# Down-weight loads split over two queues, and an earlier evacuation between retention heads

## The chip, the cores and the metric

The kernel runs on one core of a Trainium2 chip. The metric is the device time of one launch in microseconds. The three runs of the kernel before took 4532.19, 4537.35 and 4538.72 us, median 4537.35.

## The reference, cut to what matters

One inference step of a decoder layer over 576 tokens (512 prompt tokens and 8 sequences of 8 new tokens), width 2048, everything in float32. In order: a mixer (pooling groups beside four retention heads), attention over 256 memory tokens, and a channel mixer with 16384 one-neuron experts, of which every token uses 8 x 16.

```python
def retention_mixer(q, k, v, gate, pos, s0, ret_norm_g):
    ...
    qh = rotary(heads(q), pos)
    kh = rotary(heads(k), pos) * (RET_HEAD_DIM ** -0.5)
    o, s_new = retention_seq(qh, kh, vh, s0.astype(F32))
    ...
    return jax.nn.silu(gate.astype(F32)) * o, s_new

def peer(h, peer_wq, peer_subkeys, peer_u, peer_v):
    ...
        u = jnp.take(peer_u, expert, axis=0).astype(F32)
        act = jax.nn.gelu(jnp.einsum('thkd,td->thk', u, xb.astype(F32)), approximate=False)
        vv = jnp.take(peer_v, expert, axis=0).astype(F32)
        return jnp.einsum('thk,thkd->td', g * act, vv).astype(h.dtype)
```

## The kernel before, in words

**Split products.** TensorE multiplies in float32r. Each operand is split into a high part (the value rounded to float32r) and a low part (the rest), and a product is three matmuls: high by high, high by low, low by high. Weights arrive in chunks of 512 KB (128 partitions x 1024 floats). A chunk k goes through slot k % 4: a DMA fills the raw slot, ScalarE writes the high part to WS (helper `high`, L1086, the copy is recorded at L1080), and POOL subtracts to make the low part (`low_part`, L482, L484). When the low part is done, the raw slot is free for chunk k + 4. In the expert quads DVE makes the low parts of every fourth chunk, slot 3 (`low_last`, L2162, L2165).

**Retention.** Four heads, in a loop of three and a last one. TensorE projects eight blocks per head (`head_block`, L720, 96 matmuls each at L598): two of queries, two of keys, two of gates and two of values for the next head; between them stand the transposes and products of the head. ScalarE's `retention` (L1313) issues the load of the decay tables and eight loads of states, and calls `evac_head(h, 0)` (L1279), which waits for the block, evacuates it and makes the high parts of the weights two blocks on. Then it copies the transposed values, evacuates the other blocks, stores the new states, takes a square root, stores the mixer's output (L1353) and waits for its stores to land before the next head.

**Expert quads.** For most tokens (320 of 576) all experts are computed densely, four blocks of 128 experts at a time: a quad. The up weights of the first ten blocks of map rows were done earlier, so 27 quads (i = 0 to 26, QT = 27) hold 16 chunks each: 0 to 7 are up weights (uT), 8 to 15 down weights (vE), two chunks for each of four quarters q of the output. TensorE (`up`, L1016; `down`, L1033) runs four up projections, each of 48 matmuls at L598 and ended by a gelu on ScalarE, and then the down product, 16 output blocks d of 12 matmuls each at L1045. Quarter q of it waits for the low parts of chunks 8 + 2q and 9 + 2q. DVE adds each output block to X (`sums`, L2143, L2150) and, after block d = 1 and d = 9, makes the low part of chunks 11 and 15. Five more quads (27 to 31) have down weights alone.

The other 256 tokens use gathered rows: POOL issues ten gathers of 1 MB per quad (L517) in quads 0 to 25 between its low parts, and DVE multiplies and adds them (L2135).

**Queues.** SP issues every weight load, in the order of the chunks, each behind a wait for its slot (`slot_free`, L426: POOL's semaphore for slots 0 to 2, DVE's for slot 3). ScalarE's queue takes the stores of gelu values (L1551, 160 KB each, four per quad) and, in `load_next` (L1620), the two 640 KB loads for the next quad: the map of gates (PP from pmap, L1611) and the gelu values (GI, L1613). In quad 0 it takes the last stores of the map as well (L1574). POOL's queue has the gathers.

**ScalarE's order in a quad** is `ups` (L1624): for each of the four up blocks (a, e) the evacuation `gelu_out` (L1542), which also makes the high parts of the two chunks four places on (blocks (0,0), (0,1), (1,0), (1,1): chunks 4 and 5, 6 and 7, 8 and 9, 10 and 11), then the gelu store; load_next follows block (1, 0). Behind `ups` come four steps `next_highs` (L1652) with the high parts of 12 and 13, 14 and 15, and of the next quad's 0 to 3.

Of the kernel before, what the change touches and what calls it, by code (L numbers as in the profile page):

```python
# [97 lines left out]
def used(n):  # L98


    return n + 4
# [12 lines left out]
def split_uv(i12, k):  # L114

    assert k % 4 < 3
    return i12 + (H_UV + 5 + k // 4 * 3 + k % 4)


def low_uv(i4, k):  # L120

    return i4 + (k // 4 + 2)
# [37 lines left out]
def build(nc, xT, memT, w_lin, gains, consts, spoolT, sret, kcT, vc, pool_w, rot, tabs, subk, uT, vE,  # L160
          yT, npoolT_p, nret_p, mkT, mv, npoolT_s, nret_s):
    with ExitStack() as ctx:
# [3 lines left out]
        def sem(name):  # L166
            return ctx.enter_context(nc.semaphore(name))
# [50 lines left out]
        def raw(k, many, late=False):  # L218

            if late and k >= 2:  # L220
                return CS.rearrange("p a t -> p (a t)")[:, 0:HW] if k == 2 else RAW3
            return RAW[:, k, :] if k < 2 else RAWX[:, k - 2, :] if many else RAW[:, k - 2, :]
# [96 lines left out]
        S = {n: sem(n) for n in names}  # L319
# [19 lines left out]
        def _(sp):  # L339
# [98 lines left out]
                                 uT.rearrange("(b x) p w -> x b p w", x=2)[k // 4, bass.ds(4 * quad, 4), :, 256 * (k % 4):256 * (k % 4 + 1)]  # L438
                                 .rearrange("b p w -> p b w")).then_inc(S[f"raw{k % 4}"], 16)

            def load_v(i, i12, i4, first):

                for q in range(4):
                    for b in range(2):
                        k = first + 2 * q + b
                        slot_free(i12, i4, k)
                        sp.dma_start(raw(k % 4, True, True).rearrange("p (e d) -> p e d", e=2),
                                     vE[bass.ds(i * 4 + 2 * b, 2), :, 512 * q:512 * (q + 1)].rearrange("e p d -> p e d"))\
                            .then_inc(S[f"raw{k % 4}"], 16)
# [12 lines left out]
            with sp.Fori(0, QT) as i:  # L462
                for k in range(8):
                    slot_free(i * 12, i * 4, k)
                    sp.dma_start(raw(k % 4, True, True), uT[bass.ds(i * 8 + (4 * LAG + k), 1)].rearrange("a p n -> p (a n)"))\
                        .then_inc(S[f"raw{k % 4}"], 16)
                load_v(i, i * 12, i * 4, 8)
            with sp.Fori(0, NQ - QT) as i:
                load_v(i + QT, i * 6 + 12 * QT, i * 2 + 4 * QT, 0)
            for s in range(2):  # L470
# [608 lines left out]
        def _(act):  # L1079
# [163 lines left out]
            for b in range(SB):  # L1243
                r, q = b // 4, b % 4
# [34 lines left out]
            def evac_head(h, m):  # L1279
                act.wait_ge(S["used"], h * 16 + used(H_HEAD + 2 * m + 2))  # L1280
                if HEAD[m] in (4, 5):
                    pad_values(HEAD[m] - 4, m % 2)
                kw = {"scale": RD ** -0.5} if m in (2, 3) else {}
                act.activation(halves(RAWQ[:, HEAD[m], :]), pair(m % 2), ACT.Silu if m in (4, 5) else ACT.Identity, **kw)\
                    .then_inc(S["lin_evac"], 1)
                high2(h * 16 + (H_HEAD + 2 * m + 4), 2 * (m % 2))
# [26 lines left out]
            def retention(h, more):  # L1313
                act.dma_start(TAB, tabs[bass.ds(h, 1)].rearrange("a p n -> p (a n)")).then_inc(S["in_tab"], 16)
                for b in range(SB):
                    act.dma_start(SST[:, b], sret[b, bass.ds(h, 1)].rearrange("a (c p) v -> p (a c) v", p=P))\
                        .then_inc(S["in_st"], 16)
                evac_head(h, 0)
                act.wait_ge(S["vt_done"], h + 1)
                copy(VTOK[:, 0:4, :], PS[:, 2048:3072].rearrange("p (t n) -> p t n", t=4))  # L1320
                copy(VTOK[:, 4, :], bank(6, RD)).then_inc(S["v_evac"], 1)
                for m in range(1, 5):
                    if m == 4:
                        act.wait_ge(S["b_done"], h + 1)
                    evac_head(h, m)
                act.wait_ge(S["kt_done"], h + 1)
                act.wait_ge(S["in_tab"], h * 16 + 16)
                for t in range(4):
                    copy(KTOK[:, t, :], PS[:, 2048 + RD * t:2048 + RD * (t + 1)], scale=TAB[:, T_ZETA + t:T_ZETA + t + 1])
                copy(KTOK[:, 4, :], bank(6, RD)).then_inc(S["k_evac"], 1)  # L1330
                evac_head(h, 5)
                if more:
                    evac_head(h, 6)
                else:
                    act.wait_ge(S["rot_done"], RH)
                    act.wait_ge(S["used"], used(H_OUT))
                    split_early(mixT, Z_OUT, OUT_EARLY, (0, 0, 0), LO_OUT,
                                lambda b: copy_samples(h) if b == 2 else copy_outputs(h) if b == 4 else copy_state(h) if b == 7 else None)
                if more:
                    copy_samples(h)  # L1340
                    copy_outputs(h)
                    copy_state(h)
                    evac_head(h, 7)
                    store_states(h, 0, SB)
                else:
                    store_states(h, 0, 4)
                act.wait_ge(S["rvar_ready"], h + 2)
                act.activation(RSD, RVAR, ACT.Sqrt).then_inc(S["rsd_ready"], 1)
                if not more:
                    store_states(h, 4, SB)  # L1350
                act.wait_ge(S["b_done"], h + 2)
                if more:
                    act.dma_start(mixT[bass.ds(h * 2 + 8, 2)].rearrange("k p t -> p k t"), OT).then_inc(S["out_b"], 16)  # L1353
                else:
                    load_x(act, xT)
                    split_last(OT, OUT_EARLY)
                act.wait_ge(S["out_sst"], h * 128 + 128)
                act.wait_ge(S["out_spr"], h * 16 + 16)
                if more:
                    act.wait_ge(S["out_b"], h * 16 + 16)  # L1360

            for s in range(2):
# [7 lines left out]
                if s == 0:  # L1370
                    pool_out(GROUPS - 1)
            act.wait_ge(S["out_a"], 16 * GROUPS)
            with act.Fori(0, RH - 1) as h:
                retention(h, True)
            retention(RH - 1, False)
# [166 lines left out]
            def gelu_out(r, n, e):  # L1542

                act.wait_ge(S["used"], n + used(2))
                act.wait_ge(S[f"out_g{e}"], r * 16 + 16)
                act.activation(GO[:, e, :], bank(e, ND), ACT.Gelu).then_inc(S["lin_evac"], 1)  # L1546
                high2(n + 4, 2 * e, late=True)
# [24 lines left out]
            def store_map(g, first, end, done):  # L1572

                act.dma_start(pmap[first:end, :, g, :].rearrange("i p x -> p i x"),  # L1574
                              STG[(g + 1) % 2][:, 4 * first:4 * end].rearrange("p (i e) t -> p i (e t)", e=4))\
                    .then_inc(S[done], 16)
# [4 lines left out]
            for r in range(NPG):  # L1581
                g, b = r // 2, (r // 2 + 1) % 2
                if r % 2 == 0:
                    act.wait_ge(S[f"out_p{b}"], 16 + 128 * (g // 2))
                for q in range(PG // 4):
# [5 lines left out]
                    if q % 4 == 3:  # L1591
                        e = q // 4
# [27 lines left out]
            def load_next(i):  # L1620
                act.wait_ge(S["ww_ready"], i * 4)
                load_quad(i)

            def ups(i, first=False):  # L1624
                n, m, r = i * 16 + H_UV, i * 4 + B_UV, i * 2 + LAG
                act.wait_ge(S["used"], n + used(0))
                for a in range(2):
                    for e in range(2):
                        if a == 0 and not first:
                            w_highs(i, (2 * e, 2 * e + 1), WW)  # L1630
                        if first and a:
                            w_highs(i, (2 * e, 2 * e + 1), WW)
                        if first and (a, e) == (0, 1):
                            store_map(last, 8, 12, "out_r1")
                            store_map(last, 12, 16, "out_r1")
                        if first and (a, e) == (1, 0):
                            store_map(last, 24, 28, "out_r3")
                        gelu_out(r + a, n + (4 * a + 2 * e), e)
                        store_gelu(r + a, m + (2 * a + e), e)
                        if first and (a, e) == (0, 0):  # L1640
                            for sem_of_map, stores in (("out_p0", 272), ("out_p1", 272), ("out_m0", 16)):
                                act.wait_ge(S[sem_of_map], stores)
                            load_quad(0)
                        if first and (a, e) == (0, 1):
                            store_map(last, 16, 20, "out_r2")
                            store_map(last, 20, 24, "out_r2")
                        if first and (a, e) == (1, 0):
                            store_map(last, 28, 32, "out_r3")
                        if (a, e) == (1, 0) and not first:
                            load_next(i + 1)  # L1650

            def next_highs(n, q):  # L1652
                act.wait_ge(S["used"], n + used(2 * q + 2))
# [721 lines left out]
```

## Time and profile before

| what | value |
|---|---|
| median of the runs | 4537.35 us |
| profiled execution, its own time | 4544.36 us |
| its span | 4542.6 us |
| TensorE matmul busy | 4381.2 us, 96% |
| POOL busy | 2774.2 us, 61% |
| DVE busy | 2177.9 us, 48% |
| ScalarE busy | 1525.1 us, 34% |
| DMA on SP's queue (q1) | 592.77 MB, 39.9% of 16 engines |
| DMA on POOL's queue (q0) | 268.60 MB, 15.2% |
| DMA on ScalarE's queue (q10) | 168.75 MB, 10.7% |

The shares of the queues are of the time of all 16 DMA engines over the span. TensorE is the busiest engine by far, and what counts is what it waits for, stage by stage. The retention heads lie between 380 and 900 us of the span, the quads with up and down weights from some 2745 to 4350 us.

### The profile page before, as it was taken

How to read it: one execution, taken by the hardware profiler on the slowest of the kernel's cores; microseconds unless marked ns; L12 is line 12 of the kernel's file. 1: busy time of each engine (PE TensorE's matmuls, PEld its weight loads, DVE VectorE, ACT ScalarE, POOL GpSimd, SP SyncE). 2: the span in 40 equal slices, each digit the busy share in tenths (PEclk: the TensorE clock that was granted, in tenths of full speed). 3: DMA queues.
4: the chain of work that ended last, by engine and by line, in shares of the span. 5: the costliest groups of instructions: out<-in, count | busy, mean ns of one | idle time of the engine just before them, and what ended most of it. 6: DMA issues, size and time to landing. Idle time of an engine off the chain costs nothing.

```text
span 4542.6 us, 75520 instructions
## 1 busy us (share of the span) xinstructions
PE 4381.2 (96%) x28787; PEld 4141.9 (91%) x28787; DVE 2177.9 (48%) x3231; ACT 1525.1 (34%) x1921; POOL 2774.2 (61%) x1440
## 2 busy tenths in 40 slices
PE   7999999999999989999999998999999999999998
PEld 7899989899888978888888998999999999999998
DVE  3132333423102153333333565777777777777656
ACT  4422222222222244444443553333333333333332
POOL 6833222243222457777777887788788788886643
PEclk9999999999999999999999999999999999999999
DMA  6643333434564255555555559999999899999854
GB/s 228 209 95 100 111 111 106 155 105 146 196 203 168 88 177 183 182 182 181 181 181 183 187 188 341 350 359 353 354 355 358 320 357 363 358 356 347 324 190 157
DMA packets 493934, 1032.09 MB, mean 227 GB/s; under 512 B 55776, under 2 KB 285280, under 8 KB 461024
## 3 DMA queue, kind: packets, MB, share of 16 engines
q1 hardware_dynamic: 316528, 592.77, 39.9%
q0 software_dynamic: 45056, 268.60, 15.2%
q10 hardware_dynamic: 132208, 168.75, 10.7%
q8 instruction: 98, 1.61, 0.2%
q14 instruction: 44, 0.36, 0.0%
HBM read 935.26 MB, written 94.73 MB: 227 GB/s over the span
## 4 chain that ended last, share of the span: by engine, by line
PE 49%; issue 24%; POOL 17%; DMA 6%; ACT 2%; DVE 1%; POOLq 0%; ACTq 0%; SPq 0%; DVEq 0%
PE PS L598 21%; PE PS L948 15%; POOL WS L484 14%; PE PS L1045 12%; DMA RAW<-in_vE 6%; POOL AR L507 2%; ACT WS L1080 1%; POOL ROWS L517 1%; PE PS L974 0%; DMA ROWS<-in_vE,AR 0%; DMA AR<-gel 0%; DVE AR L1759 0%; DVE AR L2266 0%; PE PS L1001 0%; DVE HL L1782 0%
## 5 line engine op out<-in xcount | busy, mean ns | idle before, releaser
L598 PE MATMUL PS<-HL,WS 128*128 128x288 f32 (+2 forms) x16896 | 2394.9, 303 | 66.6 <-POOL WS L484 35.2
L598 PEld LDWEIGHTS PS<-HL,WS 128*128 128x128 f32 x16896 | 2351.7, 190 | 87.3 <-issue 30.5
L484 POOL TENSOR_TENSOR WS<-RAW,WS 128x1024 fp32r<-128x1024 f32 x600 | 1458.0, 2439 | 1418.8 <-ACT WS L1080 1416.5
L1080 ACT ACTIVATE WS<-RAW 128x1024 fp32r<-128x1024 f32 x600 | 614.8, 1055 | 1190.1 <-PE PS L598 451.6
L1045 PE MATMUL PS<-WW,WS 128*128 128x320 f32 x6144 | 927.0, 312 | 56.5 <-POOL WS L484 44.8
L1045 PEld LDWEIGHTS PS<-WW,WS 128*128 128x128 f32 x6144 | 908.6, 189 | 73.6 <-issue 36.1
L948 PE MATMUL PS<-WS,HL 128*128 128x512 f32 x3072 | 700.4, 389 | 0.0
L948 PEld LDWEIGHTS PS<-WS,HL 128*128 128x128 f32 x3072 | 575.5, 188 | 118.8
L484 POOL TENSOR_TENSOR WS<-CS,WS 128x1024 fp32r<-128x1024 f32 x200 | 482.7, 2414 | 146.9 <-ACT WS L1080 145.1
L2135 DVE SCALAR_TENSOR_TENSOR PS<-ROWS,AR,PS 128x2048 f32<-128x2048 f32 x206 | 483.3, 2346 | 9.0 <-DMA ROWS<-in_vE,AR 8.7
L2150 DVE TENSOR_TENSOR AR<-AR,PS 128x320 f32<-128x320 f32 x512 | 247.1, 483 | 317.9 <-PE PS L1045 316.7
L1080 ACT ACTIVATE WS<-CS 128x1024 fp32r<-128x1024 f32 x200 | 211.6, 1058 | 374.0 <-PE PS L1045 197.7
L484 POOL TENSOR_TENSOR WS<-AR,WS 128x1024 fp32r<-128x1024 f32 x122 | 294.4, 2418 | 56.4 <-ACT WS L1080 56.1
L1080 ACT ACTIVATE WS<-AR 128x1024 fp32r<-128x1024 f32 x240 | 251.9, 1054 | 165.9 <-PE PS L948 90.9
L2036 DVE MAX8 AR<-AR 128x8 f32<-128x128 f32 (+1 forms) x120 | 30.2, 323 | 562.7 <-ACT AR L1080 561.5
L507 POOL DMA_INDIRECT AR<-gelg,AR x256 | 254.8, 995 | 70.4 <-issue 64.3
L517 POOL DMA_INDIRECT ROWS<-in_vE,AR x206 | 217.0, 1054 | 39.3 <-issue 18.7
L1080 ACT ACTIVATE AR<-PS 128x64 f32<-128x64 f32 (+10 forms) x188 | 104.4, 600 | 348.3 <-PE PS L598 236.5
L1546 ACT ACTIVATE AR<-PS 128x320 f32<-128x320 f32 x128 | 57.0, 445 | 460.0 <-PE PS L598 449.6
L2135 DVE SCALAR_TENSOR_TENSOR PS<-AR,PS 128x2048 f32<-128x2048 f32 x50 | 117.6, 2352 | 155.0 <-DMA AR<-in_vE,AR 155.0
L2165 DVE TENSOR_TENSOR WS<-AR,WS 128x1024 fp32r<-128x1024 f32 x118 | 166.4, 1411 | 10.8 <-ACT WS L1080 10.8
L2128 DVE TENSOR_TENSOR WW<-AR,WW 128x320 fp32r<-128x320 f32 x128 | 126.2, 1019 | 8.8 <-ACT WW L1080 8.8
(220 smaller groups left out, 2274.0 us busy)
## 6 DMA issues: line engine op xcount, KB each, us to landing
RAW<-in_uT SPq DMA_DIRECT2D x256, 512.0 KB, 4.6
RAW<-in_w_lin SPq DMA_DIRECT2D x216, 512.0 KB, 3.6
CS<-in_uT SPq DMA_DIRECT2D x128, 512.0 KB, 4.7
AR<-in_uT SPq DMA_DIRECT2D x128, 512.0 KB
RAW<-in_vE SPq DMA_DIRECT2D x128, 512.0 KB, 7.9
CS<-in_vE SPq DMA_DIRECT2D x64, 512.0 KB, 4.8
AR<-in_vE SPq DMA_DIRECT2D x64, 512.0 KB
AR<-in_w_lin SPq DMA_DIRECT2D x48, 512.0 KB, 4.2
```

The lines of the kernel that those rows point to most:

```text
L484: pool.tensor_tensor(WS[:, k, 1, :], raw(k, many, late), WS[:, k, 0, :].bitcast(F32), ALU.subtract)\
L507: pool.indirect_dma_start(out=GA[:, c, k:k + 1], out_offset=None, in_=values, in_offset=at(EL[:, c, k:k + 1]))\
L517: pool.indirect_dma_start(out=ROWS[b], out_offset=None, in_=rows, in_offset=at(VI[:, c, r:r + 1]))\
L598: ins = mm(to, WS[:, slot + hf, wp, k * P:(k + 1) * P], x, start=first and (wp, xp) == (0, 0), stop=last and wp == 1, skip_group_check=True)
L948: ins = mm(tiles(bank(2 * (j % 2) + c)), HLG[:, c, xp, 2 * q + k, :], experts, start=(q, k, wp, xp) == (0, 0, 0, 0), stop=(q, k, wp) == (7 ...
L1045: ins = mm(bank(2 + d % 2, ND), WS[:, 2 * (q % 2) + b, vp, 512 * e + P * d4:512 * e + P * (d4 + 1)], W[:, 2 * b + e, wp, :], start=(b, e, ...
L1080: copy = lambda out, in_, **kw: act.activation(out, in_, ACT.Identity, **kw)
L1546: act.activation(GO[:, e, :], bank(e, ND), ACT.Gelu).then_inc(S["lin_evac"], 1)
L2128: tt(W[:, e, 1, :], GI[:, e, :], W[:, e, 0, :].bitcast(F32), ALU.subtract).then_inc(S["ww_ready"], 1)
L2135: stt(ACC, ROWS[b], GA[:, c, r:r + 1], ACC, ALU.mult, ALU.add).then_inc(S["row_done"], 1)
L2150: tt(X[:, d, 0:ND], X[:, d, 0:ND], bank(2 + d % 2, ND), ALU.add).then_inc(S["v_free"], 1)
L2165: tt(WS[:, 3, 1, :], RAW3, WS[:, 3, 0, :].bitcast(F32), ALU.subtract).then_inc(S["low_done"], 1)
```

## The change

Two edits. First, of each quad's eight loads of down weights, those of the odd chunks (9, 11, 13, 15) are no longer issued by SP but by ScalarE, on ScalarE's queue, each behind the same slot wait as before: chunk 9 in block (0, 1) of `ups`, chunks 11 and 13 at the start of block (1, 1), chunk 15 at the end. The five last quads are as before. Second, `evac_head(h + 1, 0)` is called in the retention of head h, behind the square root, instead of in head h + 1 behind its loads; for head 0 it is called ahead of the loop.

```diff
-            def load_v(i, i12, i4, first):
+            def load_v(i, i12, i4, first, parts=(0, 1)):
 
                 for q in range(4):
-                    for b in range(2):
+                    for b in parts:
                         k = first + 2 * q + b
...
-                load_v(i, i * 12, i * 4, 8)
+                load_v(i, i * 12, i * 4, 8, (0,))
...
-                evac_head(h, 0)
                 act.wait_ge(S["vt_done"], h + 1)
...
                 act.activation(RSD, RVAR, ACT.Sqrt).then_inc(S["rsd_ready"], 1)
+                if more:
+                    evac_head(h + 1, 0)
                 if not more:
                     store_states(h, 4, SB)
...
             act.wait_ge(S["out_a"], 16 * GROUPS)
+            evac_head(0, 0)
             with act.Fori(0, RH - 1) as h:
                 retention(h, True)
...
+            def load_odd(i, k):
+
+                if k == 9 or k == 13:
+                    act.wait_ge(S["split_done"], split_uv(i * 12, k - 4))
+                else:
+                    act.wait_ge(S["low_done"], low_uv(i * 4, k - 4))
+                q = (k - 9) // 2
+                act.dma_start(raw(k % 4, True, True).rearrange("p (e d) -> p e d", e=2),
+                              vE[bass.ds(i * 4 + 2, 2), :, 512 * q:512 * (q + 1)].rearrange("e p d -> p e d"))\
+                    .then_inc(S[f"raw{k % 4}"], 16)
+
             def ups(i, first=False):
...
+                        if (a, e) == (0, 1):
+                            load_odd(i, 9)
+                        if (a, e) == (1, 1):
+                            load_odd(i, 11)
+                            load_odd(i, 13)
                         gelu_out(r + a, n + (4 * a + 2 * e), e)
                         store_gelu(r + a, m + (2 * a + e), e)
...
                         if (a, e) == (1, 0) and not first:
                             load_next(i + 1)
+                load_odd(i, 15)
```

## Rows read from the trace of the kernel before

**Rows 1.** The page: chain that ended last, by line.
```profile
PE PS L598 21%; PE PS L948 15%; POOL WS L484 14%; PE PS L1045 12%; DMA RAW<-in_vE 6%; POOL AR L507 2%; ACT WS L1080 1%; POOL ROWS L517 1%; PE PS L974 0%; DMA ROWS<-in_vE,AR 0%; DMA AR<-gel 0%; DVE AR L1759 0%; DVE AR L2266 0%; PE PS L1001 0%; DVE HL L1782 0%
```
**Rows 2.** Windows: stretch, length, busy PE, PEld, DVE, ACT, POOL; clock, DMA, GB/s.
```profile
2840.00:4320.00 1480.00, 1433.97 (x9645) 1418.82 (x9644) 1085.56 (x955) 480.31 (x602) 1149.70 (x693) 1.00 0.93 350
```
**Rows 3.** Waits in 2840 to 4320 us: total us, times, longest.
```profile
PE PS L1045 <- POOL WS L484: 44.8, 49, 2.9
```
**Rows 4.** Timeline of PE in one quad: start, length, what, idle before.
```profile
3019.66 28.32 PE L598 MATMUL PS<-HL,WS 128*128 128x320 f32 x192
3048.62 14.42 PE L1045 MATMUL PS<-WW,WS 128*128 128x320 f32 x96 [0.64 <-POOL WS L484]
3064.28 14.33 PE L1045 MATMUL PS<-WW,WS 128*128 128x320 f32 x96 [1.24 <-POOL WS L484]
```
**Rows 5.** Timeline of SP in that quad: loads of chunks 11, 12 and 13.
```profile
3039.40 0.37 SPq L447 DMA_DIRECT2D AR<-in_vE  x1
3045.12 3.90 SPq L447 DMA_DIRECT2D RAW<-in_vE  x2
```
**Rows 6.** Timeline of ACT in that quad: load_next, highs of chunks 11 and 12.
```profile
3042.49 0.48 ACTq L1611 DMA_DIRECT2D AR<-pmap  x1
3043.12 0.61 ACTq L1613 DMA_DIRECT2D AR<-gel  x1
...
3049.30 1.05 ACT L1080 ACTIVATE WS<-AR 128x1024 fp32r<-128x1024 f32 x1
3056.80 1.06 ACT L1080 ACTIVATE WS<-RAW 128x1024 fp32r<-128x1024 f32 x1 [6.45 <-DMA RAW<-in_vE]
```
**Rows 7.** DMA queues in 3050 to 3056 us: packets, MB, share of 16 engines.
```profile
q0 software_dynamic: 224, 1.70, 68.6%
q1 hardware_dynamic: 239, 0.46, 20.2%
```
**Rows 8.** Timeline of PE in retention: second block, then the three gaps.
```profile
509.72 13.04 PE L598 MATMUL PS<-HL,WS 128*128 128x288 f32 x96
525.34 40.01 PE L598 MATMUL PS<-HL,WS 128*128 128x288 f32 x288 [2.58 <-POOL WS L484]
...
657.92 40.18 PE L598 MATMUL PS<-HL,WS 128*128 128x288 f32 x288 [3.82 <-POOL WS L484]
...
787.77 40.16 PE L598 MATMUL PS<-HL,WS 128*128 128x288 f32 x288 [1.95 <-POOL WS L484]
```
**Rows 9.** Timeline of ACT there: the evacuation of block 0 of head 1.
```profile
521.26 0.65 ACT L1284 ACTIVATE AR<-PS 128x576 f32<-128x576 f32 x1 [20.37 <-issue]
```
**Rows 10.** DMA issues in 2860 to 4320 us: KB each, median us to landing.
```profile
RAW<-in_vE SPq DMA_DIRECT2D x98, 512.0 KB, 10.0
...
AR<-gel ACTq DMA_DIRECT2D x25, 640.0 KB, 18.2
```
**Rows 11.** To landing: gelu load 3043.1, store 3049.1, gelu loads 2984.7 and 3217.9.
```profile
DMA to landing us min/median/max: 18.8/18.8/18.8
...
DMA to landing us min/median/max: 14.7/14.7/14.7
...
DMA to landing us min/median/max: 14.9/14.9/14.9
...
DMA to landing us min/median/max: 20.2/20.2/20.2
```
**Rows 12.** DMA in 3038 to 3044 us, all queues.
```profile
DMA packets 815, 1.73 MB, mean 288 GB/s; under 512 B 83, under 2 KB 107, under 8 KB 775
```
**Rows 13.** Timeline of DVE in that quad: low part of chunk 11.
```profile
3052.84 1.54 DVE L2165 TENSOR_TENSOR WS<-AR,WS 128x1024 fp32r<-128x1024 f32 x1
```
**Rows 14.** Quad 0: a long idle of PE (timeline), and the window behind it.
```profile
2799.26 6.39 PE L598 MATMUL PS<-HL,WS 128*128 128x320 f32 x24 [6.84 <-DVE WS L2165]
...
2800.00:2806.00 6.00, 6.00 (x27) 6.00 (x27) 3.83 (x2) 0.31 (x1) 4.80 (x4) 0.58 1.01 343
```
**Rows 15.** Timeline of ACT in quad 0: two map stores issued.
```profile
2774.54 8.60 ACTq L1574 DMA_DIRECT2D pmap<-ROWS  x2
```

## The prediction, as it was put on record

> **What bounds the kernel now.** I began with the page. TensorE is the long pole: the chain that ended last goes through three matmul lines, and the next entries, POOL's low parts (L484) and the transfer of down weights (in_vE, 6%), say what TensorE waits for [rows 1]. Most of the change lies in the expert quads, so I asked next for that stage. In 2840 to 4320 us, 25 quads, TensorE is busy 1433.97 of 1480 us at full clock, and DMA carries 350 GB/s at a share of 0.93 [rows 2]. The list of waits puts 44.8 us of TensorE's idle time there, in 49 waits, on POOL's low parts [rows 3]. The timeline of one quad shows the pattern, which repeats 25 times: 28.3 us of up projections, 0.64 us idle, half of the down product, 1.24 us idle, the other half [rows 4]. So 25 waits of 0.63 us make 15.7 us and the second kind some 29 us, or 1.2 us a quad. The first kind is the way from ScalarE's high parts of chunks 8 and 9 to POOL's two low parts with a gather between; no load is in it. The second is a late load: chunk 12, issued at 3045.12 [rows 5], lets ScalarE start only at 3056.80, after 6.45 us of waiting [rows 6]. In 3050 to 3056 us several queues share the engines: POOL's gathers have 68.6% of the time, SP's loads 20.2% [rows 7].
>
> In the retention stage the PE timeline has one gap per head: 2.58, 3.82 and 1.95 us, each after the second block of the next head, until POOL has the low part for the third [rows 8]. The ACT timeline tells why: block 0 of head 1 is done before block 1 starts at 509.72, but ScalarE evacuates it and splits the next weights only at 521.26, behind its stores and nine load issues [rows 8, 9].
>
> **Retention part.** It moves evac_head(h+1, 0) (an evacuation and two high parts) ahead of the state stores' final waits, the mixer store and the nine loads. Nothing is added. Evacuation and highs then follow block 0 at once, 12 us earlier, and POOL's low parts with them; the next raw loads, which SP issues after those, also start earlier. All three gaps go: -2.58 - 3.82 - 1.95 = -8.35 us. What is late next: ScalarE now copies the value rows after the nine issues, till about 522.6, and block 1 ends at 509.72 + 13.04 = 522.76 [rows 8], so block 1's evacuation is on time, and up to a microsecond late in the head with the 3.82 us gap, with 13 us of matmuls in hand. For head 0 the nine loads start some 14 us later. The states are first wanted after the sixth block, at 13.04 us a block; this costs nothing. Bounds -6 to -9; I take -8.4.
>
> **Expert part: what moves.** In quads 0 to 26 the loads of chunks 9, 11, 13 and 15, four of SP's sixteen 512 KB issues, go to ScalarE's queue. Bytes are the same. Each brings its slot wait with it onto ScalarE, and takes ScalarE's place in order:
> - 9 waits for POOL's low part of chunk 5, ready about 0.6 us after the gelu behind it could start. The high parts of 6 and 7 have over 1 us in hand before the fourth projection. I take 0.
> - 13 waits for the low part of 9 and holds the gelu of the fourth block for about 0.5 us. The gather ahead of POOL's next low part covers it. 0.
> - 15 waits for DVE's low part of 11, as SP did; ScalarE had a free stretch there, but only while chunk 11 is early.
> - 11 is the one that costs. Before, SP issued it at 3039.40 [rows 5], and ScalarE took it at 3049.30 without a wait [rows 6]. Now it stands behind load_next, which puts 640 KB of the map and 640 KB of gelu values on the same queue, at 3042.49 and 3043.12 [rows 6].
>
> **How late is chunk 11?** The gelu load takes 18.2 us to land (median of the 25) where an in_vE load on SP's queue takes 10.0 [rows 10]. I read the queue as being served in order, beside two others: a 160 KB store that was issued 6.0 us behind this gelu load landed 14.7 us later, at 3063.8, after the load's own 3043.1 + 18.8 = 3061.9 [rows 11]. So it took until 20.7 us after the gelu issue, though such a store has only a small transfer of its own. Chunk 11 stands in the same place with 512 KB. I take 20.0 us after the gelu issue (typical gelu landing 18.2, plus 1.8, an estimate: 0.5 MB at the 288 GB/s of 3038 to 3044 us, where SP's loads ran with hardly a gather beside them [rows 12]; the bound is 6.5, if it shares with gathers as the load of 10.0 us does). To this come the high part, 1.05 us [rows 6], DVE's low part, 1.54 us [rows 13], and the hops between, 0.4: 23.0 us.
>
> TensorE wants chunk 11 at the second quarter of the down product: 3048.62 plus half of 14.42 [rows 4] is 3055.8, 12.7 us after the gelu issue. The stall is 23.0 - 12.7 = 10.3 us a quad, in the quads with a load_next and gathers, 1 to 25.
>
> Terms with it:
> - **Clock.** The profile has one comparable gap: after 6.84 us idle, 24 matmuls took 6.39 us instead of 3.6 (a quarter of 14.42), and the granted clock in that stretch was 0.58, so most of it at 1.2 GHz, half of full speed [rows 4, 14]. That gives +2.8 a quad; 0 if the gaps stay short.
> - **Old stall.** Chunks 12 and 13 land before the late restart: -1.2.
> - **Relief.** While ScalarE stands, POOL issues no gather past the one behind chunk 10, and SP's queue carries one load less. The gelu load lands sooner by 0 to 3 us; I take 1.5.
>
> Net 10.3 + 2.8 - 1.2 - 1.5 = 10.4 us; times 25 is +260. Quad 26 has no gathers, so its loads come in time: 0. In quad 0 there is no load_next, but chunks 9 and 11 queue behind map stores; issues on ScalarE's queue already took 8.60 us for two there, so the queue pushes back [rows 15]. TensorE already waits there for other work, up to 6.84 us at a time [rows 14]. Bounds 0 and 20; I take +3, since most of that cover is as long as such a wait.
>
> **Sum.** The profiled execution took 4544.36 us (span 4542.6), 7.0 above the median of the runs, 4537.35. 4544.4 - 8.4 + 260 + 3 = 4799; on the median 4792 us.
>
> Bounds per quad: the shortest gelu landing I saw in the stage was 14.9, the longest 20.2 [rows 11]. Low: 14.9 + 1.8 + 2.6 - 12.7 = 6.6, no slow clock, less 1.2 and 1.5: 3.9 us, +98 in all. High: 20.2 + 6.5 + 3.0 - 12.7 + 2.8 = 19.8, or +495. I stay at the small transfer of its own, nearer to the low end, since the store behind the gelu load landed only 1.9 us after it.
>
> **Rivals.**
> - **The other side: chunks 12 and 13 side by side.** If chunk 11 doesn't stand behind the gelu load (the queue serves both at once), two queues of 2 KB pieces draw a larger part beside the gathers, and 12 and 13 land together. Then the second wait goes, -29 us, and with -8.4 that is 4507, 4500 on the median. It decides from the point where chunk 11 lands less than 10 us after the gelu issue (12.7 less 2.6). For it: the gathers' 68.6% against 20.2% for SP [rows 7]. Against: all gelu landings of the stage that I looked at lie between 14.9 and 20.2, and the store lands behind. The Trainium skill (DMA: Bandwidth & Descriptors, Queues, rings and completion order) says that completion is not in order per issuing engine; the store at 3063.8 against 3061.9 speaks otherwise here. Chance 0.10.
> - **Nothing in the quads.** The same 16 engines carry the same bytes at a share of 0.93 [rows 2], and chunk 11 is absorbed by slack that I misjudged. Then only the retention gaps go: 4536, 4529 on the median, 0.18% less. The Trainium skill states this as a rule (same page, Issuing engines are not separate DMA queues): issuing from several engines saves only the sequencer's time. Chance 0.05.
> - **ScalarE held at the issue.** The queue pushes back as at 2774.54 [rows 15]; chunk 13's issue and the gelu store then hold ScalarE, high part 10 comes after and chunk 14 is issued late. Another 8 to 10 us a quad: about 5020. Against: the two issues of load_next went in 0.48 and 0.61 us [rows 6]. Chance 0.07.
>
> **How the numbers follow.** My forecast has 0.78. What a measurement can tell from no change here is 0.2%, 9 us. Faster is the first rival, 0.10; same is the second, 0.05; slower is the forecast and the third, 0.85. The range starts at 4610, just under the low bound on the median (4537 - 8 + 98 = 4627), and goes to 4950, 16.5 us a quad. It leaves out both rivals below, and the thin upper end: some 0.2.
>
> **What would show it.** In the PE timeline of a quad: the first gap stays 0.6, a gap of 8 to 12 us stands 7.2 us into the down product, released by DVE's low part (L2165) or POOL, with slow matmuls after it and a granted clock below 1.00 in those windows; the gap at mid-product is gone. ScalarE's waits for in_vE loads into AR, on chunk 11, grow from about nothing to 200 us and more. The DMA share of the stage falls below 0.85, and quads last about 69 us instead of 58.6. In retention the three gaps are gone and ScalarE's first evacuation comes 0.2 us after its block. I am wrong if chunk 11 is taken within 10 us of the gelu issue, if the gelu load lands much sooner once SP's queue is lighter, or if a gap after the third block takes the place of the removed one.

## The result, and the profile after

The changed kernel takes 4811.03 us (median of 4 runs, 4806.72 to 4817.07) against 4535.9 us; the ratio is 1.0608, interval 1.0592 to 1.0624. The median of the kernel before was 4537.35 us when the prediction was made; a run has come to it since. The forecast was 4792 us.

From the page of the kernel after: the busy time of the engines, the chain that ended last, and the matmul line of the down product (count, busy us, mean ns, idle before it and its main releaser):

```profile
PE 4418.6 (92%) x28787; PEld 4181.5 (87%) x28787; DVE 2194.0 (46%) x3231; ACT 1522.5 (32%) x1921; POOL 2760.8 (57%) x1440
...
PE PS L598 20%; PE PS L1045 15%; PE PS L948 14%; DMA AR<-in_vE 10%; POOL WS L484 10%; POOL AR L507 2%; ACT WS L1080 1%; ACTq L1615 1%; PE PS L974 0%; DMA pmap<-ROWS 0%; DVE AR L2169 0%; DMA ROWS<-in_vE,AR 0%; ACTq L1613 0%; DVE AR L1778 0%; ACTq L1553 0%
...
L1045 PE MATMUL PS<-WW,WS 128*128 128x320 f32 x6144 | 972.7, 322 | 302.9 <-DVE AR L2169 286.1
```

The same line before:

```profile
L1045 PE MATMUL PS<-WW,WS 128*128 128x320 f32 x6144 | 927.0, 312 | 56.5 <-POOL WS L484 44.8
```

On the chain, the load of down weights into AR has come in with 10%: that is slot 3, chunks 11 and 15. The down product L1045 waits 302.9 us where it waited 56.5, and its matmuls themselves take 45.7 us more. (After the change DVE's lines are 19 higher: its sums are L2169, its low part of slot 3 L2184. Load_next is L1613 and L1615, the gelu L1548, the odd chunks are issued at L1633.)

The timeline of PE in one quad answers to [rows 4], with the one after it for the period:

```profile
3060.99 7.30 PE L1045 MATMUL PS<-WW,WS 128*128 128x320 f32 x48 [0.61 <-POOL WS L484]
3079.30 23.64 PE L1045 MATMUL PS<-WW,WS 128*128 128x320 f32 x144 [11.01 <-DVE AR L2169]
3102.78 28.32 PE L598 MATMUL PS<-HL,WS 128*128 128x320 f32 x192
3131.73 7.30 PE L1045 MATMUL PS<-WW,WS 128*128 128x320 f32 x48 [0.63 <-POOL WS L484]
```

The first gap is as before, 11 us stand at the second quarter (7.3 us into the down product), and the gap at mid-product is gone. The list puts the gap on DVE's sums, since the sum behind the low part was the last thing to come; what held DVE shows in ScalarE's timeline of that quad, the answer to [rows 6]:

```profile
3054.82 0.36 ACTq L1613 DMA_DIRECT2D AR<-pmap  x1
3055.34 1.40 ACTq L1615 DMA_DIRECT2D AR<-gel  x1
3056.91 0.94 ACTq L1633 DMA_DIRECT2D AR<-in_vE  x1
3061.01 0.38 ACTq L1633 DMA_DIRECT2D RAW<-in_vE  x1
3061.56 0.44 ACT L1548 ACTIVATE AR<-PS 128x320 f32<-128x320 f32 x1 [5.75 <-POOL WS L484]
3061.89 1.05 ACT L1080 ACTIVATE WS<-CS 128x1024 fp32r<-128x1024 f32 x1
3076.54 1.06 ACT L1080 ACTIVATE WS<-AR 128x1024 fp32r<-128x1024 f32 x1 [13.60 <-DMA AR<-in_vE]
```

Chunk 11 is issued at 3056.91, behind the gelu load of 3055.34, and ScalarE gets it at 3076.54, 21.2 us after the gelu issue. The waits of the stage (total us, times, longest), beside [rows 3]:

```profile
ACT WS L1080 <- DMA AR<-in_vE: 341.3, 25, 15.2
DVE WS L2184 <- ACT WS L1080: 309.1, 25, 13.7
PE PS L1045 <- DVE AR L2169: 276.4, 25, 12.4
PE PS L1045 <- POOL WS L484: 15.6, 25, 0.7
```

Twenty-five times each: load, ScalarE, DVE, TensorE, one behind the other; 276.4 / 25 is 11.06 us of gap a quad. The windows of that quad, for the clock (same columns as [rows 2]):

```profile
3061.00:3068.00 7.00, 7.00 (x48) 7.00 (x48) 3.23 (x3) 1.38 (x2) 6.20 (x5) 1.00 1.04 411
3068.00:3079.00 11.00, 0.29 (x3) 0.03 (x1) 1.37 (x2) 1.06 (x1) 0.03 (x1) 0.62 0.74 283
3079.00:3083.00 4.00, 3.69 (x14) 3.70 (x15) 3.00 (x4) 2.00 (x2) 2.28 (x1) 0.50 0.41 131
3083.00:3090.00 7.00, 7.00 (x45) 7.00 (x45) 4.03 (x5) 1.02 (x2) 4.44 (x4) 0.91 0.79 298
```

The granted clock falls to its lower level, 1.2 GHz, in the gap (0.62 on the mean of the gap), and is still there (0.50) in the first 4 us of matmuls after it. Over 2840 to 4600 us the DMA share is 0.79, under the 0.85 of the forecast, and the quad above lasts 3131.73 - 3060.99 = 70.7 us, for some 69 forecast.

In retention the three gaps of [rows 8] are gone. Head 1, from the transposes after its first block to those after its fifth, in PE's timeline of the kernel after:

```profile
504.17 1.25 PE L728 MATMUL PS<-CST,AR 128*128 128x128 f32 x10
505.18 51.43 PE L598 MATMUL PS<-HL,WS 128*128 128x288 f32 x384
556.45 1.25 PE L728 MATMUL PS<-CST,AR 128*128 128x128 f32 x10
```

That takes 52.28 us; the same stretch took 56.47 before:

```profile
508.71 1.25 PE L728 MATMUL PS<-CST,AR 128*128 128x128 f32 x10
...
565.18 1.25 PE L728 MATMUL PS<-CST,AR 128*128 128x128 f32 x10
...
522.00:532.00 10.00, 7.42 (x46) 7.19 (x45) 6.40 (x5) 5.39 (x7) 6.67 (x3) 0.83 0.56 181
```

So 4.2 us went with a gap of 2.58 us. The window of before shows where the rest comes from: around that gap the granted clock was 0.83, and in the kernel after it is 1.00 from 505 to 556 us. The other two heads give 5.6 and 3.7 us, 13.5 in all for 8.35 us of idle.

The balance of the spans, 4815.3 - 4542.6 = 272.7 us: the 25 quads with gathers and a load_next last 1770.7 us (from 2821.97 to 4592.68) instead of 1477.2 (from 2843.59 to 4320.76), +293.5 (11.7 each); quad 0 lasts 77.2 instead of 80.5, -3.3; retention -13.5; and the stretch ahead of retention, which the change doesn't touch, was 4.2 us shorter in this execution. The sum is 272.5.

### The profile page after: what moved, and what is told of

Read it like the earlier page. It is cut to its first block, busy times and chain, and to the rows that moved or that the text cites. A ratio compares the mean times of both kernels' runs of the same rounds, so it can differ in the third digit from the quotient of the medians.

```text
span 4815.3 us, 75427 instructions
## 1 busy us (share of the span) xinstructions
PE 4418.6 (92%) x28787; PEld 4181.5 (87%) x28787; DVE 2194.0 (46%) x3231; ACT 1522.5 (32%) x1921; POOL 2760.8 (57%) x1440
## 2 busy tenths in 40 slices
DMA packets 493935, 1032.10 MB, mean 214 GB/s; under 512 B 55776, under 2 KB 285280, under 8 KB 461024
## 3 DMA queue, kind: packets, MB, share of 16 engines
q10 hardware_dynamic: 161584, 225.38, 13.5%
## 4 chain that ended last, share of the span: by engine, by line
PE 50%; issue 23%; POOL 12%; DMA 11%; ACTq 2%; DVE 1%; ACT 1%; POOLq 0%; DVEq 0%
PE PS L598 20%; PE PS L1045 15%; PE PS L948 14%; DMA AR<-in_vE 10%; POOL WS L484 10%; POOL AR L507 2%; ACT WS L1080 1%; ACTq L1615 1%; PE PS L974 0%; DMA pmap<-ROWS 0%; DVE AR L2169 0%; DMA ROWS<-in_vE,AR 0%; ACTq L1613 0%; DVE AR L1778 0%; ACTq L1553 0%
## 5 line engine op out<-in xcount | busy, mean ns | idle before, releaser
L1045 PE MATMUL PS<-WW,WS 128*128 128x320 f32 x6144 | 972.7, 322 | 302.9 <-DVE AR L2169 286.1
L1045 PEld LDWEIGHTS PS<-WW,WS 128*128 128x128 f32 x6144 | 955.6, 198 | 318.9 <-DVE AR L2169 268.7
L2169 DVE TENSOR_TENSOR AR<-AR,PS 128x320 f32<-128x320 f32 x512 | 247.6, 485 | 284.6 <-PE PS L1045 284.4
L2184 DVE TENSOR_TENSOR WS<-AR,WS 128x1024 fp32r<-128x1024 f32 x118 | 181.1, 1535 | 322.4 <-ACT WS L1080 321.5
L517 POOL DMA_INDIRECT ROWS<-in_vE,AR x206 | 199.9, 970 | 39.9 <-issue 19.5
L1548 ACT ACTIVATE AR<-PS 128x320 f32<-128x320 f32 x128 | 57.0, 446 | 488.3 <-POOL WS L484 280.6
```

Source lines behind the costliest of these rows:

```text
L517: pool.indirect_dma_start(out=ROWS[b], out_offset=None, in_=rows, in_offset=at(VI[:, c, r:r + 1]))\
L1045: ins = mm(bank(2 + d % 2, ND), WS[:, 2 * (q % 2) + b, vp, 512 * e + P * d4:512 * e + P * (d4 + 1)], W[:, 2 * b + e, wp, :], start=(b, e, ...
L2169: tt(X[:, d, 0:ND], X[:, d, 0:ND], bank(2 + d % 2, ND), ALU.add).then_inc(S["v_free"], 1)
L2184: tt(WS[:, 3, 1, :], RAW3, WS[:, 3, 0, :].bitcast(F32), ALU.subtract).then_inc(S["low_done"], 1)
```

## The experiments

The kernel before, run beside these, had a median of 4542.8 us with the first four kernels below, 4544.01 us with the two that put chunk 13 on ScalarE's queue without chunk 11, and 4536.97 us with the other four. Each ratio is to the runs beside it, so ratios compare better than times.

**Each part alone.** Shown is the retention edit; the other kernel is the changed one with this edit taken back.

```diff
-                evac_head(h, 0)
                 act.wait_ge(S["vt_done"], h + 1)
...
                 act.activation(RSD, RVAR, ACT.Sqrt).then_inc(S["rsd_ready"], 1)
+                if more:
+                    evac_head(h + 1, 0)
...
+            evac_head(0, 0)
             with act.Fori(0, RH - 1) as h:
```

> The kernel before with the retention edit alone. Theory: the three gaps of 2.58, 3.82 and 1.95 us after the second block of heads 1 to 3 go and nothing else moves, so 8 us less, ratio 0.998, about 4528 us. Rival: the gaps come back later in the head (a raw load crossing the state loads, the value copy behind the nine issues), ratio within 0.0005 of 1.

4528.83 us against 4542.8, ratio 0.9974, interval 0.9962 to 0.9987: 12 us less by the ratio, 8 expected. The interval reaches from 6 to 17 us, so the runs can't tell the 8.35 us of idle from the 13.5 us of the traces. In PE's timeline of this kernel the three gaps are gone and none has come in later in the head.

> The kernel before with the expert edit alone. Theory: all of the loss is here, about 283 us, so 4819 us, and the gap of 11 us at the second quarter stands in each quad as in the changed kernel. Rival: part of the loss comes from the retention edit; then it is clearly under 4811 us.

4826.21 us, ratio 1.062 (1.0599 to 1.0641): +283 us. All of the loss is in the expert edit.

**Load_next behind chunk 15.** The changed kernel, with nothing of load_next ahead of the odd chunks:

```diff
-                        if (a, e) == (1, 0) and not first:
-                            load_next(i + 1)
+                last_up = isinstance(i, int) and i == QT - 1
+                if last_up:
+                    load_next(i + 1)
                 load_odd(i, 15)
+                if not first and not last_up:
+                    load_next(i + 1)
```

> The changed kernel with load_next issued behind chunk 15 instead of behind the third gelu (in quad 26 just ahead of 15), so that chunks 11 and 13 have no gelu load ahead of them on ScalarE's queue; all other waits and places are the same. Theory (chunk 11 is late since it stands behind the gelu load): the gap of 11 us falls to 0 to 2 us, 4500 to 4560 us. Rival A (ScalarE issues chunk 11 too late, or its slot waits cost the time): the gap stays above 8 us and the time above 4750 us. Rival B (the queue beside the gathers is slow whatever stands ahead): gap about 5 us, 4650 us.

4570.92 us, ratio 1.0061 (1.004 to 1.0082). 240 us of the loss are gone with the place of two loads. PE's timeline of a quad:

```profile
3094.08 7.30 PE L1045 MATMUL PS<-WW,WS 128*128 128x320 f32 x48 [0.61 <-POOL WS L484]
3102.09 2.03 PE L1045 MATMUL PS<-WW,WS 128*128 128x320 f32 x12 [0.71 <-DVE AR L2172]
3104.75 5.55 PE L1045 MATMUL PS<-WW,WS 128*128 128x320 f32 x36 [0.63 <-DVE AR L2172]
3110.91 14.35 PE L1045 MATMUL PS<-WW,WS 128*128 128x320 f32 x96 [0.61 <-DVE AR L2172]
```

The gap of 11 us is 0.7 in this quad, and the mid-product wait is 0.6; the last three waits are on DVE, whose low part of chunk 11 is still a little late and pushes its sums. Over 2840 to 4330 us the waits on DVE's sums come to 52.1 us in 50. Chunk 11 was issued at 3087.71 here and taken by ScalarE at 3099.32, 11.6 us later, where it took 3076.54 - 3056.91 = 19.6 us in the changed kernel. The time is 11 us over the range I had given: I had counted the gap and not DVE's sums behind it. Rivals A and B fall: the gap is neither above 8 us nor near 5. What is left, 42 us over the retention edit alone (4570.92 against 4528.83), goes with the split and load_next's late place together.

**Only chunk 11.** In the changed kernel, SP issues 9, 13 and 15 again:

```diff
-                load_v(i, i * 12, i * 4, 8, (0,))
+                load_v(i, i * 12, i * 4, 8, (11,))
...
-                        if (a, e) == (0, 1):
-                            load_odd(i, 9)
                         if (a, e) == (1, 1):
                             load_odd(i, 11)
-                            load_odd(i, 13)
...
-                load_odd(i, 15)
```

(The last argument of load_v now names the chunks that it leaves out.)

> The changed kernel with chunks 9, 13 and 15 back on SP's queue; only chunk 11 on ScalarE's, behind load_next. Theory: one chunk carries the loss; gap at the second quarter 9 to 11 us a quad, 4770 to 4810 us. Rival (the four loads together choke ScalarE's queue, or the waits for 9, 13 and 15 hold ScalarE): the gap is half or less, under 4680 us.

4814.17 us, ratio 1.058 (1.0551 to 1.061): the same loss with one load moved, 4 us over the expected range. ScalarE's timeline (L1617 is the gelu load here, L1635 chunk 11):

```profile
3060.90 0.41 ACTq L1617 DMA_DIRECT2D AR<-gel  x1
3061.50 0.61 ACTq L1635 DMA_DIRECT2D AR<-in_vE  x1
...
3082.17 1.06 ACT L1082 ACTIVATE WS<-AR 128x1024 fp32r<-128x1024 f32 x1 [15.23 <-DMA AR<-in_vE]
```

Chunk 11 comes 21.3 us after the gelu issue, as with all four moved, and TensorE's waits on DVE's sums are 237.2 us in 21 quads, 11.3 each. So 9, 13 and 15 on the queue, and their slot waits on ScalarE, are not what costs.

**Chunk 11 ahead of load_next, 13 behind it.**

```diff
                         if (a, e) == (1, 1):
-                            load_odd(i, 11)
+                            if first:
+                                load_odd(i, 11)
                             load_odd(i, 13)
...
                         if (a, e) == (1, 0) and not first:
+                            load_odd(i, 11)
                             load_next(i + 1)
```

> The changed kernel with only chunk 11's issue put ahead of load_next; 13 and 15 stay behind it. Theory: the gap at the second quarter falls from 11 to 1 or 2 us, as in the run with load_next last, but chunk 13 now is the one behind the gelu load (landing about 21 us after its issue, wanted about 19 after it, less 1 for the high and 5 for POOL's two low parts), so a new gap of 4 to 7 us stands ahead of the third quarter: 4650 to 4720 us. Rival (what counts is only that chunk 11 is issued 2 us earlier, the queue is not in order): both gaps about 1 us, under 4600 us.

4682.21 us, ratio 1.0315 (1.0298 to 1.0332). The gap moved to the third quarter:

```profile
3059.69 2.02 PE L1045 MATMUL PS<-WW,WS 128*128 128x320 f32 x12 [0.97 <-DVE AR L2171]
3062.35 5.54 PE L1045 MATMUL PS<-WW,WS 128*128 128x320 f32 x36 [0.64 <-DVE AR L2171]
3071.91 15.64 PE L1045 MATMUL PS<-WW,WS 128*128 128x320 f32 x96 [4.02 <-POOL WS L484]
```

ScalarE took chunk 13 at 3068.31 in this quad, 20.3 us after the gelu issue at 3048.02. Chunk 11, now ahead of load_next, was issued at 3045.05 and taken at 3056.92, 11.9 us later. What stands behind the gelu load is late, whichever chunk it is.

**Chunks 9 and 13 on ScalarE's queue, 11 and 15 on SP's.** As in the kernel with only chunk 11, with (9, 13) for (11,) and the issues of 9 and 13 left in their places.

> The changed kernel with chunks 11 and 15 back on SP's queue, 9 and 13 on ScalarE's, 13 behind load_next. Theory: no gap at the second quarter; chunk 13 lands about 21 us after the gelu issue and makes a gap of 4 to 6 us ahead of the third quarter instead of the 1.2 us of before, so 4600 to 4660 us. Rival (only four loads together overload ScalarE's queue, one behind load_next does little): under 4560 us.

4709.92 us, ratio 1.0359 (1.0343 to 1.0375), 50 us over the top of what I expected. The mechanism was as expected, the size was not:

```profile
3051.92 14.43 PE L1047 MATMUL PS<-WW,WS 128*128 128x320 f32 x96 [0.64 <-POOL WS L486]
3072.99 16.05 PE L1047 MATMUL PS<-WW,WS 128*128 128x320 f32 x96 [6.63 <-POOL WS L486]
```

The gap is 6.6 us, and 96 matmuls behind it take 16.05 us instead of 14.33. In this quad ScalarE got chunk 13 at 3069.38, 23.2 us after the gelu issue at 3046.22, where I had put 21. Part of the difference is the gelu load itself, whose median to landing is 20.9 us here; the rest was not tried. (Chunk 13 is issued 5.7 us behind the gelu load here, at 3051.95, and chunk 11 was 1.6 us behind it in the changed kernel.)

**TensorE kept busy through the gap.** 72 matmuls on values at rest, ahead of the wait for chunk 11:

```diff
...
                 for q in range(4):
+                    if filler is not None and q == 1:
+                        pe.wait_ge(S["lin_evac"], filler)
+                        for _ in range(72):
+                            mm(bank(0, ND), HLD[:, 0, 0, 0:P], HLD[:, 0, 0, :], start=True, stop=True, skip_group_check=True)
                     for b in range(2):
                         weights_uv(i12, i4, first + 2 * q + b)
...
```

(The call of `down` passes `filler` in quads 0 to 25.)

> The changed kernel with 72 extra matmuls of 320 columns (10.6 us) on values at rest, into a bank that is free, at the second quarter of quads 0 to 25; their output is overwritten. Theory: they fill the gap, the granted clock stays at 1.00, and the 2.1 us that the matmuls behind each gap take longer come back: 45 to 55 us less than the changed kernel, 4755 to 4770 us. Rival (the matmuls behind the gap are slow for another reason, such as DVE's late sums): no faster than the changed kernel, or slower by what the filling overhangs.

4781.85 us, ratio 1.0534 (1.0517 to 1.0552), 29 us less than the changed kernel though TensorE does more, and 12 us above the range that I had given.

```profile
3070.08 10.72 PE L1040 MATMUL PS<-HL 128*128 128x320 f32 x72
3081.76 2.02 PE L1049 MATMUL PS<-WW,WS 128*128 128x320 f32 x12 [0.96 <-DVE AR L2174]
3084.42 19.62 PE L1049 MATMUL PS<-WW,WS 128*128 128x320 f32 x132 [0.64 <-DVE AR L2174]
...
3079.00:3083.00 4.00, 3.04 (x21) 2.78 (x20) 2.92 (x3) 2.01 (x2) 0.00 (x0) 1.00 0.19 70
```

The window behind the gap has the full clock now (0.50 before). Of the 2.1 us by which the matmuls were slower, 29 / 25 = 1.2 us come back; a new wait of 0.64 us for DVE's sum shows, which the slow clock had hidden. So the clock's part is shown, but it is smaller than the 45 to 55 us that I expected.

**Without the gathers.** In the changed kernel POOL counts up the gathers' semaphores instead of issuing them:

```diff
-                pool.indirect_dma_start(out=ROWS[b], out_offset=None, in_=rows, in_offset=at(VI[:, c, r:r + 1]))\
-                    .then_inc(S[f"in_row{b}"], 16)
+                pool.sem_inc(S[f"in_row{b}"], 16)
```

> The changed kernel without POOL's row gathers (their semaphores are counted up by POOL itself; the products for the 256 gathered tokens are made from whatever the buffers hold). Theory: the loads on ScalarE's queue are late since each of their pieces takes its turn beside the 8 KB pieces of a gather; alone on the engines the gelu load lands in 7 to 9 us and chunk 11 within 12, so the gap of 11 us is gone: 4460 to 4510 us. Rival (the order in the queue alone makes it late): the gap stays above 5 us, above 4650 us.

4450.13 us, 0.9803 of the kernel before (0.9787 to 0.982), 10 us below the expected range; it moves 268 MB less (763.65 instead of 1032.10). The gap is gone, and in the quad from 3040 us on chunk 11 is taken 8.9 us after the gelu issue. The gelu load, in its old place ahead of chunk 11, lands in 5.8 us instead of 19.9, where I had expected 7 to 9 (DMA issues, KB each, median to landing; first without gathers, then the changed kernel):

```profile
AR<-gel ACTq DMA_DIRECT2D x27, 640.0 KB, 5.8
```

```profile
AR<-gel ACTq DMA_DIRECT2D x24, 640.0 KB, 19.9
```

So the order in the queue alone doesn't make chunk 11 late. It takes both: a load ahead, and the gathers beside it. The run takes away 268 MB as well as the large packets, so it doesn't tell whether the amount or the size of the gathers' packets counts.

**Two tries at a faster kernel.** First the retention edit, with load_next one block later (in block (1, 1), behind the store), all weights on SP's queue:

> The retention edit alone, with load_next one block later (behind the fourth gelu and its store), all weights on SP's queue. Theory: half of the 1.2 us waits at mid-product are chunks 12 and 13 beside load_next's 1.3 MB; with it issued 7 us later they fall, 4500 to 4520 us. Rival (the gathers alone set how late 12 and 13 are, or chunks 14 and 15 are late instead): 4520 to 4535 us, no difference to the retention edit alone.

4534.64 us, ratio 0.9999 (0.9988 to 1.0009), inside the rival's range: no gain over the retention edit alone (0.9974), but a small loss. TensorE's waits on POOL's low parts in the stage did fall, from 47.5 us in the retention edit alone to 32.1, but 12.8 us of waits on DVE's sums came in. Then the same kernel with chunk 13 alone on ScalarE's queue, load_next behind it (shown against the kernel before, without the retention edit and the body of load_odd):

```diff
-                load_v(i, i * 12, i * 4, 8)
+                load_v(i, i * 12, i * 4, 8, (13,))
...
+                        if (a, e) == (1, 1):
+                            load_odd(i, 13)
                         gelu_out(r + a, n + (4 * a + 2 * e), e)
                         store_gelu(r + a, m + (2 * a + e), e)
...
-                        if (a, e) == (1, 0) and not first:
+                        if (a, e) == (1, 1) and not first:
                             load_next(i + 1)
```

> The retention edit, chunk 13 alone on ScalarE's queue, and load_next behind it (after the fourth gelu and its store). Theory of a gain: 12 and 13 move side by side with no gelu load ahead of either, the mid-product wait of 1.2 us goes in most quads, 4495 to 4515 us. Rival (the wait is set by the gathers' share, and DVE's late sums or chunks 14 and 15 take its place): 4520 to 4540 us, no better than the retention edit alone.

4509.12 us, ratio 0.9926 (0.9912 to 0.994), in the range given for the gain, and below both kernels. PE's timeline:

```profile
3076.63 14.42 PE L1047 MATMUL PS<-WW,WS 128*128 128x320 f32 x96 [0.62 <-POOL WS L486]
3091.25 7.29 PE L1047 MATMUL PS<-WW,WS 128*128 128x320 f32 x48 [0.20 <-POOL WS L486]
3099.06 7.32 PE L1047 MATMUL PS<-WW,WS 128*128 128x320 f32 x48 [0.52 <-DVE AR L2167]
```

The mid-product wait is 0.2 us instead of 1.2. Part of it comes back at the last quarter, where DVE's sums are now late. In ScalarE's timeline of that quad the high parts of chunks 12 and 13 follow each other closely, where 3.83 us lay between them before (3056.80 and 3060.63):

```profile
3084.04 1.06 ACT L1082 ACTIVATE WS<-RAW 128x1024 fp32r<-128x1024 f32 x1 [4.38 <-PE PS L1047]
3085.29 1.06 ACT L1082 ACTIVATE WS<-RAW 128x1024 fp32r<-128x1024 f32 x1 [0.18 <-DMA RAW<-in_vE]
```

Chunk 13 was issued at 3076.75 on ScalarE's queue, 3.6 us behind chunk 12 on SP's. The kernel of the first try differs from this one in chunk 13's queue alone, so 0.9999 to 0.9926 is what that one load gives, once load_next stands behind it. This is what the split over two queues can give: chunks 12 and 13 side by side, with nothing ahead of either.

## Why the prediction was right, point by point

- **Chunk 11 behind load_next.** Right in place, cause and size. The forecast had the gelu issue plus 20.0 us for the landing and 23.0 for TensorE's restart; ScalarE took the chunk at 21.2, and TensorE went on at 3079.30 - 3055.34 = 24.0. The gap was put at 10.3 us and is 11.06 (mean of 25). One thing in the picture of the queue was too simple: it is served in order by landings, not by bytes (last section).
- **Relief of 1.5 us.** Wrong in sign. The gelu load was to land sooner with SP's queue lighter and POOL held; its median went from 18.2 to 19.9 us. The gathers did not let up: POOL issued three more behind the gelu issue (3057.49, 3061.02, 3065.82) and they had 51.1% of the engines' time from 3055.3 to 3075.3 us, against 53.9% from 3043 to 3062 before. And what SP's queue gave up, ScalarE's queue took: 963 packets fell to 544 on the one, 949 rose to 1292 on the other. That this is why the gelu load was not relieved is read from the traces, not tried.
- **Clock.** Put at 2.8 us a quad from quad 0. The trace gives 23.64 us for 144 matmuls where 14.34 us for 96 make 21.5, so 2.1; over the whole run the line's busy time grew by 45.7 us, 1.8 a quad, and the run that kept TensorE busy won 1.2.
- **Old stall.** Right: POOL's waits fell from 44.8 us in 49 to 15.6 in 25, so the second kind is gone, 1.2 us a quad.
- **Per quad** the forecast was 10.4 us; the periods show 11.7 (11.06 + 2.1 - 1.2 = 12.0 by the terms of one quad, with no relief), the runs of the expert edit alone 283 / 25 = 11.3.
- **Retention.** Mechanism right, the sum mis-sized: -8.4 forecast, -13.5 in the traces, about -12 in the runs. I had counted the idle time and left the slower matmuls behind each gap out, though I charged the very same thing to the quads.
- **Quad 0.** +3 forecast, -3.3 measured, so wrong in sign. A new wait of 1.17 us on POOL's low parts stands ahead of the down product, but the waits on DVE's sums within it fell from 7.1 to 5.2 us; why was not tried.
- **Cancelling.** The 19 us between 4792 and 4811 are in part luck, since the errors cancel: the quads cost 33 us more than forecast (293 to 260), retention gave 5 more, quad 0 was 6 better. In the profiled execution 4 us more went ahead of retention, where nothing was changed.
- **The rivals.** That chunks 12 and 13 side by side would win was true by itself, and the last kernel shows it (0.9926 against 0.9999 without the move); it could not come out while chunk 11 stood behind the gelu load. That an own queue saves only issue time, which the Trainium skill gives as a rule (DMA: Bandwidth & Descriptors, Issuing engines are not separate DMA queues), doesn't hold here in either direction: one load on another queue cost 285 us in one place (4814.17 against 4528.83 with the retention edit alone) and, with load_next behind it, gained 0.7% in another. That completion is not in order per issuing engine, which the Trainium skill says (same page, Queues, rings and completion order), did not help either: in one quad of each of the six kernels with gathers and a chunk behind the gelu load, the chunk came 20 to 23 us after the gelu issue. ScalarE held at its issues showed only as 1.4 and 0.9 us for two of them. The slot waits of chunks 9 and 13 held a gelu for 1.3 and 1.1 us (5.14 and 5.75 us of idle where 3.88 and 4.61 stood), for 0.6 and 0.5 forecast; the kernel with chunk 11 alone, which has neither, lost as much.

What stays open: how the waits on DVE's sums could be brought down in the fastest kernel, and why load_next's new place, moved alone, lost a little.

## What to carry to other kernels

Before a load is moved to another engine's queue, look at what is issued just ahead of it there, and at that load's time to landing: beside the gathers the moved one came later still. Then compare with when its consumer, and whatever that consumer blocks in order, needs it. A queue of its own does pay where it lets two urgent loads go side by side, with the one that can wait issued behind them. And a gap of 2 us or more on TensorE cost more than its idle time here (13.5 us for 8.35 of idle in retention, some 2 us on top of each 11 in the quads), since the matmuls behind it run at the lower clock for some microseconds.

## What the runs showed of the hardware that was not expected

The shares beside a gather. In 3062 to 3074 us of the changed kernel all three queues had work, and the engines' time went so (packets, MB, share of 16 engines):

```profile
q0 software_dynamic: 450, 3.14, 64.0%
q10 hardware_dynamic: 501, 0.88, 19.6%
q1 hardware_dynamic: 443, 0.87, 19.4%
```

The three queues moved about the same number of packets, 443 to 501, so the bytes follow the size of a packet: some 7 KB for the gathers, 2 KB for the loads. The same shows with two queues in [rows 7] (224 and 239 packets). A gelu load with 640 KB of the map ahead of it lands in 5.8 us without the gathers and in 19.9 beside them.

In order by landings, not by bytes. From the gelu issue at 3055.34 to its landing 20.0 us later, ScalarE's queue moved this (3055.3 to 3075.3 us, packets, MB, share of 16 engines):

```profile
q10 hardware_dynamic: 1292, 2.40, 33.6%
```

The gelu store ahead, the map and the gelu load have 1.47 MB together, so more than 0.9 MB of the 1.05 MB of chunks 11 and 13 had been moved before the gelu load had landed. Yet ScalarE took chunk 11 only 1.2 us after that landing. What held the last piece of each load the trace doesn't show.
